# TensorE reads the weight columns of every projection last to first

## The reference

```python
def reference(x, ...):
    h = x
    # layer 0: stick-breaking attention, layer 1: chunked gMLP; each followed by a SwiGLU FFN
    h = h + stick_breaking_mixer(rmsnorm(h, sb_norm), w_qkv, w_o)     # 2048 x 6144, 2048 x 2048
    h = h + swiglu_ffn(rmsnorm(h, ffn_norm[0]), w_gate_up, w_down)    # 2048 x 11264, 5632 x 2048
    h = h + chunked_gmlp_mixer(rmsnorm(h, gm_norm), w_in, ..., w_o)   # 2048 x 4096, 2048 x 2048
    h = h + swiglu_ffn(rmsnorm(h, ffn_norm[1]), w_gate_up, w_down)
    return rmsnorm(h, final_norm)
```

## Time and profile before

| | |
|---|---|
| median of 3 runs | 2097.78 us (2097.42 to 2098.17) |
| span of the profiled execution, first to last instruction | 2097.8 us |
| the profiled execution's own time | its span; it is counted in the same way as the runs |
| TensorE busy | 2088.2 us (100%), 9281 matmul records |
| VectorE, ScalarE busy | 1430.7 us (68%), 1013.1 us (48%) |
| read from HBM | 399.55 MB, 191 GB/s over the span |

### The profile page before, as it was taken

One profiled execution on the slowest core, in us unless ns is written; L12 is line 12 of the kernel. 1 busy time (PEld: TensorE's weight loads), 2 busy tenths in 40 slices (PEclk: granted clock), 3 DMA queues, 4 the chain that ended last, 5 costly groups with the idle time before them and its releaser, 6 DMA issues.

```text
span 2097.8 us, 27159 instructions
## 1 busy us (share of the span) xinstructions
PE 2088.2 (100%) x9281; PEld 1729.4 (82%) x9281; DVE 1430.7 (68%) x1822; ACT 1013.1 (48%) x1285; POOL 16.4 (1%) x30
## 2 busy tenths in 40 slices
PE   9999999999999999999999999999999999999998
PEld 7888888888888888888888888888888888888887
DVE  6787777867666676665557887877666676664444
ACT  6577765544444444444445444554444444444443
POOL 1000000000000000000000000000000000000000
PEclk9999999999999999999999999999999999999999
DMA  8555554666666666555566665566666666655554
GB/s 264 179 179 170 181 189 167 198 196 192 191 190 198 191 193 195 192 191 196 194 192 209 190 200 183 190 190 201 192 189 198 192 193 194 190 194 198 192 191 150
DMA packets 207419, 402.47 MB, mean 192 GB/s; under 512 B 12336, under 2 KB 13056, under 8 KB 206976
## 3 DMA queue, kind: packets, MB, share of 16 engines
q1 hardware_dynamic: 206496, 398.11, 61.1%
q0 software_dynamic: 688, 3.18, 0.4%
q10 hardware_dynamic: 176, 0.40, 0.1%
HBM read 399.55 MB, written 2.10 MB: 191 GB/s over the span
## 4 chain that ended last, share of the span: by engine, by line
PE 99%; issue 0%; DMA 0%; DVE 0%; ACT 0%; POOLq 0%; POOL 0%; DVEq 0%; SPq 0%
PE acc L1085 64%; PE acc L1091 32%; PE tp L1156 0%; PE tp L1176 0%; PE acc L1106 0%; PE acc L1107 0%; PE acc L1108 0%; PE tp L1302 0%; DMA h<-in_x 0%; PE tp L1116 0%; PE acc L1345 0%; PE acc L1344 0%; PE acc L1343 0%; PE acc L1143 0%; PE tp L1136 0%
## 5 line engine op out<-in xcount | busy, mean ns | idle before, releaser
L654 DVE TENSOR_TENSOR w_lo<-raw,w_hi 128x1024 fp32r<-128x1024 f32 x750 | 916.0, 1224 | 584.9 <-ACT w_hi L348 581.1
L348 ACT ACTIVATE w_hi<-raw 128x1024 fp32r<-128x1024 f32 x750 | 792.9, 1060 | 922.4 <-PE acc L1091 917.2
L1085 PE MATMUL acc<-w_hi,xT 128*128 128x512 f32 x4032 | 998.7, 390 | 0.0
L1085 PEld LDWEIGHTS acc<-w_hi,xT 128*128 128x128 f32 x4032 | 756.0, 188 | 155.9
L1091 PE MATMUL acc<-w_lo,xT 128*128 128x512 f32 x2016 | 539.2, 389 | 0.0
L1091 PEld LDWEIGHTS acc<-w_lo,xT 128*128 128x128 f32 x2016 | 378.6, 188 | 78.5
L1085 PE MATMUL acc<-w_hi,hid_hi 128*128 128x512 f32 x944 | 368.7, 391 | 0.0
L1085 PE MATMUL acc<-w_hi,hid_lo 128*128 128x512 f32 x944 | 367.6, 389 | 0.0
L1091 PE MATMUL acc<-w_lo,hid_hi 128*128 128x512 f32 x944 | 252.5, 389 | 0.0
L1091 PEld LDWEIGHTS acc<-w_lo,hid_hi 128*128 128x128 f32 x944 | 177.3, 188 | 36.7
L1085 PEld LDWEIGHTS acc<-w_hi,hid_hi 128*128 128x128 f32 x944 | 177.3, 188 | 36.8
(11 more groups left out here) (115 smaller groups left out, 477.6 us busy)
## 6 DMA issues: line engine op xcount, KB each, us to landing
raw<-in_ffn_w_gate_up SPq DMA_DIRECT2D x352, 512.0 KB, 4.5
raw<-in_ffn_w_down SPq DMA_DIRECT2D x176, 512.0 KB, 3.6
raw<-in_sb_w_qkv SPq DMA_DIRECT2D x95, 512.0 KB, 4.3
raw<-in_gm_w_in SPq DMA_DIRECT2D x64, 512.0 KB, 4.4
raw<-in_sb_w_o SPq DMA_DIRECT2D x32, 512.0 KB, 4.1
raw<-in_gm_w_o SPq DMA_DIRECT2D x32, 512.0 KB, 4.0
h<-in_x SPq DMA_DIRECT2D x3, 512.0 KB, 7.6
gain_bc<-in_gm_v_norm POOLq DMA_DIRECT2D x1, 1024.0 KB, 6.1
```

What stands on the lines that cost most here:

```text
L348: nc.scalar.activation(w_hi[:, p % RING], raw[:, p % RING], ACT.Copy).then_inc(hi_ready, 1)
L654: nc.vector.tensor_tensor(w_lo[:, p % RING], raw[:, p % RING], w_hi[:, p % RING].bitcast(f32), ALU.subtract).then_inc(lo_ready, 1)
L1085: nc.tensor.matmul(acc_at(chunk, r), part[:, kt, rs], w_hi[:, p % RING, k], start=(kt == 0 and part is hi), stop=False)
```

## The change

Two helpers are new. `acc_back` is `acc_at` with the 512 columns of the same bank in reverse order; `back` gives the weight's 512 columns in reverse order. Each projection matmul now uses both, in all three places (`piece` in both branches, and the row-wise end), so that column 511 is read first and written first, and each column lands where it did before. The stationary operands are as before. Four of TensorE's five hardware loops over chunks become Python loops, whose bodies stand in the program once for each chunk; the loop of the feed-forward chunks (L1257) stays. No other engine's program changes.

```diff
+        def acc_back(chunk, rt):
+
+            return acc[:, ::-1][:, bass.ds((2 * RT - 1 - rt) * CH - half(chunk) * (RT * CH), CH)]
+
+        def back(t, slot, k):
+
+            return t[:, slot, k, ::-1]
...
                             for part in (hi, lo):
-                                nc.tensor.matmul(acc_at(chunk, r), part[:, kt, rs], w_hi[:, p % RING, k],
+                                nc.tensor.matmul(acc_back(chunk, r), part[:, kt, rs], back(w_hi, p % RING, k),
                                                  start=(kt == 0 and part is hi), stop=False)
...
-                            last = nc.tensor.matmul(acc_at(chunk, r), hi[:, kt, r * P:(r + 1) * P],
-                                                    w_lo[:, p % RING, k], start=False, stop=(kt == K - 1))
+                            last = nc.tensor.matmul(acc_back(chunk, r), hi[:, kt, r * P:(r + 1) * P],
+                                                    back(w_lo, p % RING, k), start=False, stop=(kt == K - 1))
...
-            with pe.Fori(1, ND) as j:
+            for j in range(1, ND):
                 qkv_round(j)
...
             def residual_rest(which, base, hi, lo, first):
-                with pe.Fori(first, ND) as c:
+                for c in range(first, ND):
...
-            with pe.Fori(2, ND) as c:
+            for c in range(2, ND):
                 pe.wait_ge(gelu_ready, c - 1)
...
-            with pe.Fori(1, ND) as c:
+            for c in range(1, ND):
                 u_chunk(c, False)
```

More of the change, by code:

```diff
@@ L1104, in piece @@
                         rs = slice(r * P, (r + 1) * P)
[L1105 to L1108, removed]
+                        dst = acc_back(chunk, r)
+                        nc.tensor.matmul(dst, hi[:, kt, rs], back(w_hi, p % RING, k), start=(kt == 0), stop=False)
+                        nc.tensor.matmul(dst, hi[:, kt, rs], back(w_lo, p % RING, k), start=False, stop=False)
+                        last = nc.tensor.matmul(dst, lo[:, kt, rs], back(w_hi, p % RING, k), start=False,
                                                 stop=(kt == K - 1))
@@ L1336, in _ @@
                 rs = slice(r * P, (r + 1) * P)
-                dst = acc_at(1, r)
+                dst = acc_back(1, r)
                 for t in range(ROWWISE, 2 * PF):
@@ L1342, in _ @@
                         kt = (t - PF) * KP + k
-                        nc.tensor.matmul(dst, hid_hi[:, kt, rs], w_hi[:, t % RING, k], start=False, stop=False)
-                        nc.tensor.matmul(dst, hid_hi[:, kt, rs], w_lo[:, t % RING, k], start=False, stop=False)
-                        last = nc.tensor.matmul(dst, hid_lo[:, kt, rs], w_hi[:, t % RING, k], start=False,
+                        nc.tensor.matmul(dst, hid_hi[:, kt, rs], back(w_hi, t % RING, k), start=False, stop=False)
+                        nc.tensor.matmul(dst, hid_hi[:, kt, rs], back(w_lo, t % RING, k), start=False, stop=False)
+                        last = nc.tensor.matmul(dst, hid_lo[:, kt, rs], back(w_hi, t % RING, k), start=False,
                                                 stop=(kt == KF - 1))
```

## The result

| | before | after |
|---|---|---|
| median of 4 runs | 2097.82 us | 2157.07 us (2156.68 to 2157.30) |
| ratio, 95% interval | | 1.0281 (1.0267 to 1.0296) |
| span of the profiled execution | 2097.8 us | 2155.5 us |

The change makes the kernel slower by 59 us, 2.8%. The forecast was 2018 us in a range of 1998 to 2150: the wrong sign, and outside the range.

What follows compares the result with a forecast made beforehand. The prediction took TensorE's pace of 226.7 ns in 9024 projection matmuls as the bound. From 2097.8 us it took 80 for the direction and 0 for the loops, giving 2018 us, range 1998 to 2150.

Steps and rivals of the forecast that it cites:

- What bounds the kernel: Whole kernel: TensorE's 9024 projection matmuls at 226.7 ns each, 2045.4 us, 97.5% of the span.
- The loops: TensorE's loops written out: more code fetched, but hidden by the queue of matmuls; 0 us, with 2 us either way.
- The direction: Projection matmuls' moving read and accumulator write reversed: gap falls from 226.7 to 217.8 ns, 80 us less.
- 12 becomes 4, and they meet a third as often: Moving read against stationary load in SBUF: closing rate, in bytes a cycle, falls; excess 13.3 ns becomes 4.4.
- rival of more frequent meetings: Projection matmuls: if the stationary tile is read upwards, the turned read meets it more often, so slower; chance 0.18.
- milder form: Projection matmuls: the disturbed pace becomes lasting, 232 ns, 2150 us; chance 0.10 for up to 2150.
- the disturbed rows: Projection matmuls at the start and after a head's plain float32 matmuls, starting 230 to 232 ns apart.
- main form: Projection matmuls: three times the meetings, 40 ns for 13.3, gap 253 ns, 2339 us; chance 0.08 beyond 2150.
- the hint I set against it: Stationary load: skill's fast-load chunks step minus 32 columns and DoubleRow takes its first weight reversed, suggesting a downward read.
- The fixed price: Projection matmuls: the excess is fixed per matmul, gap stays 226.7 ns, 2097.8 us; chance 0.27 together with no effect.
- Who is next if TensorE gains: ScalarE, VectorE and weight DMA with a piece every 2.61 us: none becomes the bound.
- Lost pairing: Projection matmuls' backward reads or writes go one element at a time: 433 ns, some 3960 us; chance 0.12.

Runs made afterwards that it cites:

- the bench: Kernels of TensorE matmuls alone, the trunk's computation left out, segments varying read order, offset and tile size; float32r 128x512 forwards 226.7 ns, backwards 233.3 ns.
- m3_bench: Third kernel of matmuls alone, 40 to a segment, varying line order and stationary tiles; 96 columns keeping the last column's place 9.07 us, the first's 9.20 us.
- e5_shift_up: The kernel before, all forwards, with lead_in 32 bytes longer, moving the region of hid_hi and hid_lo off w_hi's 512-byte grid; 2116.83 us, ratio 1.0092.
- e2_write_back: The changed kernel with the weight read forwards again, only the accumulator written last to first; 2097.89 us, ratio 1.0001.
- m2_bench: Second kernel of matmuls alone, 48 to a segment, accumulator forwards, varying column groups, alternating directions, shifts and column numbers; groups of 4 descending 11.21 us.

## Why the prediction was wrong, point by point

**What bounds the kernel** was right: TensorE's pace in the projection matmuls and nothing else. The change was worth 9024 times what it did to 226.7 ns (60 us against the measured 59), with the tail and the other engines out of it.

**The loops** were right: 0 us, shown by itself (2097.84 us), and the instruction queue grew by a quarter as said.

**The direction: the step that failed** is "12 becomes 4, and they meet a third as often". Its ground, that the excess has to do with how the moving read and the stationary tile stand to each other, was borne out: 32 bytes of shift in one operand cost 19 us in the full kernel, the bench does it with all other engines silent, and a shift of both by 32 elements takes back what the shift of one costs. What failed is the arithmetic made of it. I took the excess to be a count of meetings over the whole length of both tiles, set by their rates and the sign of the step. Three results speak against such a count: stationary tiles of a half and of an eighth of the columns, both ending on the 256-byte grid, did not lower the excess (230 and 231 ns); turning the order of the blocks, which turns the overall direction, left 226.7; and a change of order inside 64 bytes raised the pace to 266.7. What the runs show in its place: for 512 moving columns the excess goes with the order of the 16-byte lines within a 256-byte block and with the place of the stationary tile against it. With the ascending order and the tiles on one 256-byte grid the pace settles at 226.7 ns. The full reversal settles at 233.3, 6.7 more where the prediction had 8.9 less, and the shifts of the stationary tile that are no multiple of 64 elements settle between 228 and 234, most of them near 233.

**The mechanism of the loss** was the rival of more frequent meetings, its milder form: "the phase of the disturbed rows becomes the lasting one: 232 ns, 2150 us". The gap is 233.3 and lasts. The rival's main form, three times the meetings and 253 ns, failed with the same count: the excess went from 13.3 to 20.0 ns. The term that was mis-sized there is 5.8 ns a matmul, taken from a few uneven starts after a disturbance; measured are 6.6. That is why the range, which ended at this rival's 2150, missed 2157 by 7 us. That the milder price came so near is partly luck: the uneven starts after a disturbance happen to average close to the settled backward pace. The point that I named in favour of this rival, that the present pace is that of a settled phase, was worth more than the hint I set against it. A kernel whose pace depends on a relative address, and whose `lead_in` keeps that address, stands at a chosen good point; a change of order leaves it, and I gave that too little weight. The Trainium skill's hint ("TensorE: Matmul & The Clock Gate", "Weight-path perf modes — Fast Weight Load (FWL) and DoubleRow") was about the direction of a load. Whether it holds for this load stays open, since no run turned the stationary tile; that the place of its last column decides (`m3_bench`, 226.7 against 230 ns) points that way. If it does hold, turning the moving read to run the same way as the load still raised the excess.

**The fixed price** was wrong as a rival for this change, since the pace moved. The Trainium skill's rule beside it, in "Step-by-step: what each phase is for" of "TensorE: Matmul & The Clock Gate", that loading the next stationary tile takes nothing from the running matmul's reads, does not fit `e5_shift_up` or the bench, where moving the stationary tile alone changes the matmuls' pace by 6.7 ns. The 215.8 ns that the same page of the Trainium skill gives is met in bf16, by the row of 8.63 us for 40 matmuls.

**Who is next if TensorE gains** was not put to the test, as TensorE lost.

**Lost pairing** was wrong on both sides. Writing the accumulator with a step of minus one costs nothing (2097.89 us), and neither does reading pairs or single 16-byte lines of the moving operand backwards; reading all of it backwards costs 6.7 ns and not 206. The Trainium skill, "PSUM — Partial Sum Buffer", "Specifications (TRN2)", says that any pattern that is not contiguous slows matmuls significantly; a reversed bank did not, in `e2_write_back`. A little over two cycles a column do appear in the bench, at a moving step of 2: 21.76 us for 48, 453 ns each.

**What stays open.** No row names the stall. Not settled are what makes up the 13.3 ns forwards, of which some 8 go when the moving operand reads a single column, why so many orders settle at the same 233.3 ns, why turning 64 bytes is so much dearer than turning 256, why 504 moving columns take as long as 512, and why very small stationary tiles are slower.

## What to carry to other kernels

A TensorE at 100% is not a TensorE at its peak: take the distance between starts, compare it with columns over clock, and treat the excess as a quantity with a cause. For float32r at full rate, with 512 moving columns, that excess depends on how the moving tile's 16-byte lines are ordered within 256 bytes and on its address against the stationary tile's; ascending reads on one 256-byte grid were the best found, and a small bench of segments on lines of their own finds such a point in one run. Measure the shape that you use: with 256 columns the direction cost nothing. When a pace is that of a settled phase at a chosen address, price a change of order with the pace of the rows where the phase is off, in full, before hoping for a gain.

## What the runs showed of the hardware that I had not expected

- float32r matmuls of 512 columns settle at 226.7 ns forwards, 233.3 backwards and 266.7 with groups of 16 turned, the same in the bench and in the full kernel (2098, 2157 and 2457 us).
- Moving the stationary tile up by 4, 8 or 16 elements against the moving one costs 6.7 ns a matmul, by 64 elements nothing; moving the other tile up by 16 costs less, 11.01 us for 48 (`m2_bench`, L121). `lead_in` is worth 19 us against a shift of 8 elements, for the matmuls that it concerns.
- Fewer stationary columns never made the matmuls faster: 226.7 ns with 96 to 124 columns whose last one keeps its place, 230 with 64 and 231 with 16. With 96 columns that keep the first place instead it is 230.
- bf16 and plain float32 matmuls of 512 columns have no direction: 215.8 ns both ways, and 20.60 us a segment both ways.
- Mixing the directions, eight forwards and four backwards, costs some 20 ns a piece beyond the directions' own pace (2131.8 us with a third of them turned); changing with every matmul costs nothing beyond it (230 ns).
